# First mixer's head norm on all partitions: sums by products with a matrix of ones, square roots and reciprocals on whole PSUM banks, gate tile 14 moved ahead of two transposes

## The reference, cut to what matters

```
oa = diff_attention(qa, ka, va, lam)                      # 8 heads x 128 features, per token
oa = rmsnorm(oa, g_subln) * (1 - lambda_init)             # the head norm: mean of squares over the 128 features of a head
od = sum over 3 groups of softmax(lse) * dilated_window_attention(...)   # 4 heads x 64
merged = sigmoid(ga) * (oa @ w_proj_a) + sigmoid(gb) * (od @ w_proj_b)
x = x + rmsnorm(merged @ w_out, g_post_mix)
```

## Time and profile before

| what | value |
|---|---|
| median of three runs | 1776.18 us |
| the profiled execution's own time | 1773.73 us |
| its span (first to last instruction) | 1771.9 us |
| PE busy | 1737.5 us, 98% of the span |
| DVE busy | 1203.9 us, 68% |
| ACT busy | 839.3 us, 47% |
| POOL busy | 844.6 us, 48% |

### The profile page before, as it was taken

The page is one execution under the profiler, slowest core; times in us unless marked ns, Lnnn a source line. Parts: engine busy times, 40 slices in busy tenths (PEclk is TensorE's granted clock), DMA queues, the critical chain, the costliest instruction groups (busy, mean ns, idle before and its releaser), DMA issues.

```text
span 1771.9 us, 33827 instructions
## 1 busy us (share of the span) xinstructions
PE 1737.5 (98%) x12106; PEld 1594.4 (90%) x12106; DVE 1203.9 (68%) x2217; ACT 839.3 (47%) x1263; POOL 844.6 (48%) x348
## 2 busy tenths in 40 slices
PE   9999999999999999989999999999999999999998
PEld 8999888888989998978999999999998888889997
DVE  6765787475266667688566999999985555544444
ACT  5444532556554446575344555444443333344444
POOL 4666586743856665730026788100024444444442
PEclk9999999999999999999999999999999999999999
DMA  7655544532545554533544555433345555555553
GB/s 245 207 190 183 179 167 155 179 108 85 177 153 184 185 189 150 172 131 119 177 169 167 178 189 167 154 124 128 124 151 189 189 189 189 189 178 186 186 186 118
DMA packets 85763, 296.20 MB, mean 167 GB/s; under 512 B 10484, under 2 KB 14549, under 8 KB 85542
## 3 DMA queue, kind: packets, MB, share of 16 engines
q1 hardware_dynamic: 82688, 290.82, 49.2%
q10 hardware_dynamic: 2982, 4.09, 0.8%
HBM read 293.83 MB, written 1.05 MB: 166 GB/s over the span
## 4 chain that ended last, share of the span: by engine, by line
PE 71%; issue 10%; POOL 10%; DVE 7%; ACT 1%; DMA 0%; POOLq 0%; SPq 0%; DVEq 0%; ACTq 0%
PE ps L1974 12%; PE ps L1976 12%; PE ps L1975 11%; POOL ring_lo L563 10%; PE ps L2505 7%; PE ps L2506 7%; PE ps L2507 7%; PE ps L2547 3%; PE ps L2093 2%; PE ps L2213 2%; PE ps L2094 2%; PE ps L2095 2%; PE ps L2038 1%; DVE ring_lo L1241 1%; DMA ring<-in_stream 0%
## 5 line engine op out<-in xcount | busy, mean ns | idle before, releaser
L1976 PE MATMUL ps<-h_hi,ring_lo 128*128 128x256 f32 (+1 forms) x2432 | 685.3, 282 | 0.0
L563 POOL TENSOR_TENSOR ring_lo<-ring,peer_split 128x1024 fp32r<-128x1024 f32 x128 | 315.8, 2467 | 463.9 <-ACT peer_split L693 458.2
L1976 PEld LDWEIGHTS ps<-h_hi,ring_lo 128*128 128x128 f32 x2432 | 459.0, 189 | 0.0
L563 POOL TENSOR_TENSOR ring_lo<-ring,main_hi 128x1024 fp32r<-128x1024 f32 x116 | 291.4, 2512 | 198.8 <-ACT main_hi L693 178.2
L693 ACT ACTIVATE peer_split<-ring 128x1024 fp32r<-128x1024 f32 x256 | 270.2, 1056 | 206.0 <-PE ps L2507 206.0
L563 POOL TENSOR_TENSOR ring_lo<-ring,more_hi 128x1024 fp32r<-128x1024 f32 x87 | 224.1, 2575 | 210.4 <-ACT more_hi L693 205.6
L1974 PE MATMUL ps<-h_hi,peer_split 128*128 128x256 f32 x1024 | 292.3, 285 | 3.4 <-POOL ring_lo L563 2.0
L1975 PE MATMUL ps<-h_lo,peer_split 128*128 128x256 f32 x1024 | 287.8, 281 | 0.0
L693 ACT ACTIVATE main_hi<-ring 128x1024 fp32r<-128x1024 f32 x159 | 167.4, 1056 | 118.5 <-DMA ring<-in_stream 88.3
L1974 PE MATMUL ps<-h_hi,main_hi 128*128 128x256 f32 (+1 forms) x776 | 222.2, 286 | 0.5 <-ACT arena L1010 0.4
L1975 PE MATMUL ps<-h_lo,main_hi 128*128 128x256 f32 (+1 forms) x776 | 218.4, 281 | 0.0
(11 more groups left out here) (461 smaller groups left out, 3358.5 us busy)
## 6 DMA issues: line engine op xcount, KB each, us to landing
ring<-in_stream SPq DMA_DIRECT2D x550, 512.0 KB, 3.3
x<-in_x SPq DMA_DIRECT2D x4, 256.0 KB, 5.7
arena<-in_decay ACTq DMA_DIRECT2D x4, 256.0 KB
arena<-in_keys ACTq DMA_DIRECT2D x1, 1024.0 KB, 5.6
out<-h SPq DMA_DIRECT2D x4, 256.0 KB, 2.9
arena<-in_mask ACTq DMA_DIRECT2D x1, 768.0 KB, 6.7
aux<-in_dft ACTq DMA_DIRECT2D x4, 72.0 KB
arena<-in_filter_w ACTq DMA_DIRECT2D x1, 260.0 KB
```

What stands on the lines that cost most here:

```text
L563: nc.gpsimd.tensor_tensor(ring_lo[:, c % NS, :], ring[:, c % NS, :], hi_part(c).bitcast(F32), ALU.subtract).then_inc(lo_pool, 1)
L1976: return M(out, w_lo, parts[0], start=False, stop=stop, skip_group_check=True)
```

## The change

It has four parts.

1. Head sums: PE multiplies the full 128x128 matrix of ones (stationary) with each head's squares (moving, 256 tokens), eight products of 128x256 in 32-bit floats. Each puts the head's sum on all 128 partitions at once, into acc(hd). They stand together behind dl_turn(3) and wait for ACT's copies out of those banks.
2. Roots: ACT loads the square-root table by a 128x1 operation behind dl_copy(3), then takes the roots in PSUM, one instruction of 128x1024 for each half (four heads, two banks), with scale and bias inside it; the bias is a new constant, one more 128x1 memset on POOL at the program's start.
3. Reciprocals: DVE takes them in PSUM on 128x1024 for each half, and multiplies four heads at a time into oa (128x1024). dl_take(1) now stands behind both halves. The 16 spreading products, the 128x16 steps and their semaphores are gone; proj_b waits for both halves (oa_ready 2).
4. Gate tile 14 on PE stands ahead of dl_turn(2) and dl_turn(3) instead of behind them, and gate tile 13 has nothing between its products. On DVE gate_scale(14) is the next instruction behind gate_scale(13).

```diff
@@ ACT @@
-            act_e.wait_ge(sub_var, 1)
-            A(sub_root_t, sub_root_t, ACT.Sqrt).then_inc(sub_std, 1)
+            sqrt_table()
+            f = (1.0 - LAMBDA_INIT) ** -2
+            for half in range(2):
+                act_e.wait_ge(sub_sum, half + 1)
+                A(head_roots(half), head_roots(half), ACT.Sqrt, scale=f / P, bias=eps_sub).then_inc(sub_std, 1)
             for hd in range(DA_H):
-                act_e.wait_ge(oa_ready, hd + 1)
+                act_e.wait_ge(oa_ready, hd // 4 + 1)
                 A(oa_parts[:, 0, hd, :], oa[:, hd, :], ACT.Copy).then_inc(oa_hi, 1)
@@ DVE @@
             gate_scale(DA_H + 5)
 
-            dve.wait_ge(sub_sum, 1)
-            f = (1.0 - LAMBDA_INIT) ** -2
-            V.tensor_scalar(sub_root_t, ps[:, 7, 0:2 * DA_H], f / P, f * EPS, ALU.mult, ALU.add).then_inc(sub_var, 1)
-            dve.wait_ge(sub_std, 1)
-            V.reciprocal(sub_rstd_t, sub_root_t).then_inc(sub_rstd, 1)
             gate_scale(14)
+            for half in range(2):
+                dve.wait_ge(sub_std, half + 1)
+                heads = slice(4 * half, 4 * half + 4)
+                link(V.reciprocal(head_roots(half), head_roots(half)))
+                V.scalar_tensor_tensor(oa[:, heads, :], ot[:, heads, :], col("g_subln"), head_roots(half), ALU.mult, ALU.mult).then_inc(oa_ready, 1)
             dl_take(1)
-            for hd in range(DA_H):
-                dve.wait_ge(sub_spread, hd // 2 + 1)
-                V.scalar_tensor_tensor(oa[:, hd, :], ot[:, hd, :], col("g_subln"), acc(hd), ALU.mult, ALU.mult).then_inc(oa_ready, 1)
@@ PE @@
-            def head_sums(hd):
-                pe.wait_ge(sub_sq, hd + 1)
-                if hd == 0:
-                    pe.wait_ge(od_ready, 1)
-                for t in range(2):
-                    c = 2 * hd + t
-                    ins = M(ps[:, 7, c:c + 1], merged[:, hd, t * P:(t + 1) * P], ones[:, 0:1], start=True, stop=True)
-                if hd == DA_H - 1:
-                    ins.then_inc(sub_sum, 1)
+            def head_sums():
+                pe.wait_ge(sub_sq, DA_H)
+                for hd in range(DA_H):
+                    if hd % 6 == 0:
+                        pe.wait_ge(dl_tcopied, 3 + hd // 6)
+                    ins = M(acc(hd), ones, merged[:, hd, :], start=True, stop=True)
+                    if hd % 4 == 3:
+                        ins.then_inc(sub_sum, 1)
@@ PE, dl_values @@
                 if pair:
-                    pe.wait_ge(sub_var, 1)
+                    pe.wait_ge(od_ready, 1)
@@ PE, the order @@
             dl_values(0)
-            gate_tile(DA_H + 5, head_sums)
+            gate_tile(DA_H + 5)
+            gate_tile(14)
             dl_turn(2)
             dl_turn(3)
-            gate_tile(14)
+            head_sums()
             dl_values(1)
-            pe.wait_ge(sub_rstd, 1)
-            for hd in range(DA_H):
-                for t in range(2):
-                    c = 2 * hd + t
-                    ins = spread(acc(hd)[:, t * P:(t + 1) * P], sub_rstd_t[:, c:c + 1], P)
-                if hd % 2:
-                    ins.then_inc(sub_spread, 1)
+            gate_tile(15)
+
             pe.wait_ge(od_ready, DIL_H // 2)
-            gate_tile(15)
-
-            pe.wait_ge(oa_ready, DA_H)
+            pe.wait_ge(oa_ready, 2)
```

More of the change, by code:

```diff
@@ L169, in build @@
         root_t, rstd_t = stat[:, 0, 0:3], stat[:, 1, 0:3]
-        sub_root_t, sub_rstd_t = stat[:, 0, 16:32], stat[:, 1, 16:32]
         small = sb("small", [P, 256])
@@ L276, in build @@
         warm = arena[:, 3328:3328 + T]
-        eps_half, eps_full, spare = small[:, 240:241], small[:, 241:242], small[:, 242:243]
+        eps_half, eps_full, spare, eps_sub = (small[:, n:n + 1] for n in range(240, 244))
         s = Space(arena, first + 4 * T)
@@ L348, in build @@
         rstd_ready, rstd_spread = sem("rstd_ready"), sem("rstd_spread")
-        sub_rstd, sub_spread = sem("sub_rstd"), sem("sub_spread")
         early_hi, early_lo, early_scaled = sem("early_hi"), sem("early_lo"), sem("early_scaled")
@@ L367, in build @@
         dl_turned, dl_tcopied, dl_out, od_ready = sem("dl_turned"), sem("dl_tcopied"), sem("dl_out"), sem("od_ready")
-        sub_sq, sub_sum, sub_var, sub_std, oa_ready = sem("sub_sq"), sem("sub_sum"), sem("sub_var"), sem("sub_std"), sem("oa_ready")
+        sub_sq, sub_sum, sub_std, oa_ready = sem("sub_sq"), sem("sub_sum"), sem("sub_std"), sem("oa_ready")
         sg_ready, merged_ready = sem("sg_ready"), sem("merged_ready")
@@ L393, in acc, with head_roots @@
             return ps[:, n // 2, (n % 2) * T:(n % 2 + 1) * T]
+        def head_roots(half):
+            return ps[:, 2 * half:2 * half + 2, :].rearrange("p b (a t) -> p (b a) t", t=T)
         def token_tiles(w):
@@ L589, in _ @@
             pool.wait_ge(eps_set, 4)
+            nc.gpsimd.memset(eps_sub, (1.0 - LAMBDA_INIT) ** -2 * EPS).then_inc(eps_set, 1)
+            pool.wait_ge(eps_set, 5)
             nc.gpsimd.memset(hdn[64:65, :], 1.0).then_inc(iota_ready, 1)
@@ L1976, in product, with tile @@
                 return M(out, w_lo, parts[0], start=False, stop=stop, skip_group_check=True)
-            def tile(c, out, parts, ready=None, beside=None):
+            def tile(c, out, parts, ready=None):
                 low(c)
@@ L1984, in tile @@
                     ins = product(out, c, k * P, parts(k), k == 0, k == KT - 1)
[L1985 to L1988, removed]
                 return ins
@@ L2224, in da_score, with gate_tile @@
                 ins.then_inc(da_scores, 1)
-            def gate_tile(n, beside=None):
+            def gate_tile(n):
                 if n >= 2:
                     pe.wait_ge(gate_copied, n - 1 if n < DA_H or DA_H < n < 13 else n)
-                ins = tile(START["gates"] + n, gate_bank(n), h_real, None, beside)
-                if not beside:
-                    ins.then_inc(chunk_done, 1)
+                tile(START["gates"] + n, gate_bank(n), h_real).then_inc(chunk_done, 1)
             def da_values(hd):
```

## The result

The changed kernel took 1794.53 us, the median of four runs (1792.72 to 1796.77), against 1777.18 for the kernel before beside it: a ratio of 1.0091 (95% interval 1.0076 to 1.0106), that is 16 us slower by the ratio and 17.35 between the medians. The forecast was 1792.7, in a range of 1786 to 1800.

What follows compares the result with a forecast made beforehand. The prediction took PE, busy 98% of the span, to bound the kernel, with DVE setting points in this stretch. Proj_b 13.7 us late plus 2.8 for the clock gave 16.5 us, on the median 1776.18 1792.7 us, range 1786 to 1800.

Steps and rivals of the forecast that it cites:

- Step 1: PE's gate tile 14, moved ahead, waits 6.3 us for gate_scale(13) on DVE; proj_b 1.9 us late from this alone.
- Step 2: On DVE, two reciprocals of 128x1024 at 6.9 us each (bounds 1.22 and 16.2) make proj_b start 13.7 us late.
- Step 3: PE's clock falls to half behind the pauses ahead of tile 14 and proj_b: 1.4 us lost each, 2.8 together.
- The sum: Proj_b 13.7 us late plus 2.8 us for PE's clock: 16.5 us slower.
- What was costed at nothing: POOL's memset, the 128x16 steps, the splits of oa, weight splits and sigmoids would neither cost nor gain time.
- the delay stays to the end: Behind proj_a everything hangs on PE's own progress, so no later wait takes back the delay.
- A: Rival, chance 0.16: DVE's wide reciprocal costs a quarter more, 8.3 ns a column, 8.6 us a half; 1796.1 us.
- B: Rival, chance 0.05: DVE's reciprocal streams at other operations' pace, 1.22 us a half; proj_b 2.3 us late, 1778.5 us.
- C: Rival: PE's clock doesn't fall (1789.9 us) or falls for longer, up to 9.5 us more; within the forecast case's 0.74.
- D: Rival, chance 0.03: tile 14 doesn't wait, DVE reaching gate_scale(13) early, 1786.5 us; elsewhere, time from first pair's values to proj_b.

Runs made afterwards that it cites:

- e10: Changed kernel with each reciprocal on 512 columns in the place of 1024, the other tokens multiplied by the root; ratio 1.0067 to the kernel before.
- e2: Changed kernel with each reciprocal of 128x1024 replaced by a plain copy of the same size; ratio 1.0026 to the kernel before.
- e8: Changed kernel with 50 products of 128x256 ahead of gate tile 14 and 80 behind tile 15, keeping PE busy; ratio 1.0075 to the kernel before.
- e3: Changed kernel with gate tile 14 back behind the transposes and copies in the place of the reciprocals; ratio 1.0005 to the kernel before.
- e5: Changed kernel with DVE's gate_scale(13) moved between dl_max(3) and dl_probs(2), PE's order as changed; ratio 1.0066 to the kernel before.
- e4: Kernel before with only gate tile 14 moved ahead of dl_turn(2) and dl_turn(3), old head norm untouched; ratio 1.0035 to the kernel before.
- e7: Changed kernel with gate_scale(13) early, dl_take(1) ahead of the products into oa, logarithm and exponential on ACT for root and reciprocal; ratio 1.0010 to the kernel before.
- e6: Kernel before, old norm reordered: gate_scale(13) early, head sums in one piece, tile 14 ahead of transposes, spreading ahead of values, dl_take(1) later; ratio 1.0031 to before.
- e1: Changed kernel with gate tile 14 put back behind dl_turn(2) and dl_turn(3), ahead of the head sums; ratio 1.0069 to the kernel before.

## Why the prediction was right, and where its sizes were off

- Step 1, gate tile 14 waits: right. The pause was 6.16 us for 6.3, released by gate_scale(13). The sums took 3.6 us as 8 products (432.19 - 428.56) for 3.4.
- Step 2, the reciprocal: right, 6.57 us for 6.9. Its own narrow rows led to it; the bounds of 1.22 and 16.2 us would not have. e10 shows that DVE's time there goes into proj_b's start one to one (6.4 us less on DVE, 7.1 less in D, of which tile 14's clock is 0.7), and e2 that the pause goes when the reciprocals do.
- Step 3, the clock: the mis-sized term. The mechanism was right; the size, 1.4 us for each pause, was taken from one case. Tile 14 lost 5.3 - 3.0 = 2.3 and proj_b 9.0 - 6.7 = 2.3, together 4.6 for 2.8; e8 took back 4.5. The half clock stayed for 5.2 us behind the first restart and for 2 x (1 - 0.71) x 7.7 = 4.5 behind the second, where the one case in the earlier trace rows had 2.8. The size is not fixed by the kernel: e10, with the same first pause, lost 1.6 us in tile 14 for 2.3.
- The sum: 16.5 worked out, 17.2 in E. D without the clock's 2.3 is 12.7 late for 13.7; of that 1.0 the reciprocals' shorter time is 0.7. The two errors, 1.8 us too little for the clock and 1.0 too much for the rest, partly cancelled, and that the forecast came within 2 us of the median is in part luck.
- What was costed at nothing: e3 bears it out, with E 31.8 for 31.9 and a ratio of 1.0005 (0.9996 to 1.0014). And the delay stays to the end, as was said: from the start of proj_a to the end of the span it is 1333.5 us before, 1335.9 in the changed kernel and 1333.3 in e3, so no later wait took any of it back.
- The rest of the difference between the profiled executions (1795.05 - 1773.73 = 21.3) is not the stretch: 1.7 us lay ahead of it, and 2.4 us behind it, where there were two more stretches of half clock. In the ten experiments' traces the first pair's values started between 405.73 and 410.13 us, with the same work ahead of them, so the 1.7 us are no mark of the change. The medians differ by 17.35.
- The rivals. A, a dearer wide reciprocal, falls: 6.25 ns a column between 512 and 1024. The repeat count of 8 that the Trainium skill gives ("VectorE: DVE Perf Modes", First, the fixed hardware budget) made 8.3 ns an estimate; the trace has 6.25, and the measurement decides. B, a reciprocal at the pace of other operations, falls by e2: the copy took 1.23 us, the reciprocal 6.57. C came true on its longer side. D didn't come: tile 14's wait was there. The reason given against it, that DVE's queue is full, holds only for the order as written: put ahead of the last probabilities in e5, gate_scale(13) ran at 415.68 us.

## What to carry to other kernels

A product with a matrix of ones saves the spreading, but it makes every partition hold every value, so that what follows works on 2048 columns where 16 did: cost the slowest operation behind it at its own pace a column, read from its own rows, before trading. An instruction moved ahead on an in-order engine brings its wait with it, in front of work that was ready; look at what releases it and where that stands on the other engine. Work freed ahead of a point that another engine sets is not time gained. And a gain or loss of 1 or 2 us is not to be read from one profiled execution, since the clock can add as much by chance: time several.

## What was not expected of the hardware

Half clock came behind pauses much shorter than the 4.27 us of the earlier trace rows: 2.43 us in e4, 2.54 us in e5 and e7. In e6 it came with no pause, behind 3.8 us of products with a single column. And it doesn't come every time: behind 3.72 us it came in e1 and not in e3, with the same program up to there. In the changed kernel it also came in two places far from the change, whose pauses the kernel before passed at full clock: from 521.0 us, behind one of 0.84 us, and from about 787 us, behind one of 2.13 us. In windows of the changed kernel:

```profile
518.00:521.00 3.00, 2.11 (x16) 1.94 (x17) 2.69 (x6) 1.55 (x2) 0.00 (x0) 1.00 0.00 0
521.00:524.40 3.40, 3.40 (x18) 3.40 (x18) 1.23 (x3) 0.53 (x2) 0.00 (x0) 0.50 0.10 27
...
787.00:789.00 2.00, 2.00 (x8) 1.71 (x7) 1.27 (x3) 1.43 (x4) 0.00 (x0) 0.56 0.00 0
789.00:791.00 2.00, 2.00 (x13) 2.00 (x12) 1.87 (x2) 2.00 (x3) 0.00 (x0) 0.58 0.62 174
```

Each takes up to 1.7 us (3.4 us at half), and such a loss can come or stay away from one execution to the next; what decides on which pause it falls stays open here.
